# Two token groups through a two-layer encoder trunk: gathered tokens first, dense tokens behind them in plain fp32

## The reference

```python
# layer 0: gMLP over chunks of 128 tokens
u, v = split(gelu(rms_norm(h) @ w_in));  v = rms_norm(v)
h = h + (u * (ws . v + bs)) @ w_out
h = h + peer(rms_norm(h))
k, v = split(rms_norm(h) @ w_kv)                  # shared keys and values
# layer 1: sliding-window attention with sinks and ALiBi
h = h + attention(rms_norm(h) @ w_q, k, v) @ w_o
h = h + peer(rms_norm(h))
y = rms_norm(h)

def peer(x):                                      # 8 heads, 16384 experts of one neuron
    sc = (x @ w_q) . sub_keys                     # 2 halves x 128 keys for each head
    top 16 of each half, their 16 x 16 sums, top 16 of these -> idx, gate = softmax
    return sum over 8 x 16 of gate * gelu(exp_u[idx] . x) * exp_v[idx]
```

## Time and profile before

| | |
|---|---|
| time, median of 3 runs | 3579.42 us (3577.8 to 3583.21) |
| the profiled execution | 3584.95 us, its span 3583.1 us |
| busy: PE, DVE, ACT, POOL | 3009.3, 2532.4, 761.0, 1066.6 us |
| mean granted clock of PE | 0.893 |
| DMA | 1001.05 MB, of it gathers 671.13 MB |
| first and second expert stage, first one-hot to last gather step | 516 to 1735 us, 2336 to 3551 us |

### The profile page before, as it was taken

How to read it: one execution, slowest core, us unless ns; L and a number is a source line. 1 busy time by engine, 2 the same in 40 slices (tenths; PEclk the granted TensorE clock), 3 DMA queues, 4 the chain that set the end, 5 groups by cost and what they waited for, 6 DMA issues and landing times. The chain is left out here.

```text
span 3583.1 us, 48006 instructions
## 1 busy us (share of the span) xinstructions
PE 3009.3 (84%) x17918; PEld 2642.4 (74%) x17918; DVE 2532.4 (71%) x5382; ACT 761.0 (21%) x2270; POOL 1066.6 (30%) x872
## 2 busy tenths in 40 slices
PE   7889769999999997665587988599999999985664
PEld 6789759888878886444574888489888888864453
DVE  3346898777777778676635268987777777777776
ACT  2223212111111111111225232222111111111111
POOL 3233122222222223333344331122222222333331
PEclk9989879999999998777785899799999999987777
DMA  3122359999999999999420122599999999999996
GB/s 131 57 74 76 132 207 368 366 390 384 386 373 386 381 375 350 365 350 359 155 64 1 40 94 76 188 352 354 386 387 385 382 384 389 389 345 353 361 352 227
DMA packets 146430, 1001.05 MB, mean 279 GB/s; under 512 B 16976, under 2 KB 18320, under 8 KB 30816
## 3 DMA queue, kind: packets, MB, share of 16 engines
q0 software_dynamic: 92160, 671.13, 48.7%
q1 hardware_dynamic: 50400, 317.74, 23.3%
q10 hardware_dynamic: 3712, 10.26, 0.8%
HBM read 991.33 MB, written 7.86 MB: 279 GB/s over the span
## 5 line engine op out<-in xcount | busy, mean ns | idle before, releaser
L1100 POOL DMA_INDIRECT gat<-uvg,idxg x640 | 752.6, 1176 | 1879.5 <-DVE acc L1389 1829.5
L585 PE MATMUL bank<-a,V 128*128 128x256 f32 x4096 | 1004.8, 408 | 260.2 <-DVE a L1373 260.2
L1381 DVE CUSTOM_DVE_ANT_0 gat<-gat,xrow 128x1024 f32<-128x1024 f32 x640 | 782.0, 1222 | 556.7 <-DMA gat<-uvg,idxg 552.4
L585 PEld LDWEIGHTS bank<-a,V 128*128 128x128 f32 x4096 | 842.9, 207 | 405.3 <-issue 273.9
L572 PE MATMUL bank<-xd,U 128*128 128x256 f32 x4096 | 954.1, 393 | 0.7 <-DMA U<-uvd 0.7
L572 PEld LDWEIGHTS bank<-xd,U 128*128 128x128 f32 x4096 | 801.0, 198 | 112.5 <-DMA U<-uvd 0.8
L1389 DVE SCALAR_TENSOR_TENSOR acc<-gat,wgt,acc 128x1024 f32<-128x1024 f32 x640 | 819.2, 1280 | 28.3 <-ACT wgt L910 27.9
L908 ACT ACTIVATE act<-dot 128x1 f32<-128x1 f32 x640 | 129.2, 202 | 1850.7 <-DVE dot L1381 1850.4
L559 PEld LDWEIGHTS bank<-B,oneA 128*128 128x128 f16 x4096 | 279.6, 151 | 81.8 <-issue 46.7
L559 PE MATMUL bank<-B,oneA 128*128 128x32 f16 x4096 | 286.0, 246 | 59.7 <-DVE B L1362 37.0
L1064 POOL TENSOR_TENSOR wl<-raw,wh 128x1024 fp32r<-128x1024 f32 x76 | 182.9, 2408 | 364.3 <-ACT wh L856 135.0
(11 more groups left out here) (144 smaller groups left out, 2441.1 us busy)
## 6 DMA issues: line engine op xcount, KB each, us to landing
U<-uvd SPq DMA_DIRECT2D x128, 1024.0 KB, 8.6
V<-uvd SPq DMA_DIRECT2D x128, 1024.0 KB, 8.9
raw<-lin SPq DMA_DIRECT2D x76, 512.0 KB, 3.5
gat<-uvg,idxg POOLq DMA_INDIRECT x640, 8.5
hsp<-h ACTq DMA_DIRECT2D x2, 2304.0 KB, 6.9
hx<-hsp SPq DMA_DIRECT2D x2, 2304.0 KB, 15.4
h<-xT SPq DMA_DIRECT2D x8, 288.0 KB, 7.5
yT<-h SPq DMA_DIRECT2D x8, 288.0 KB, 2.3
```

What stands on the lines that cost most here:

```text
L585: mm = pe.matmul(bank[b][:, TD * (d % 2):TD * (d % 2) + TD], V[:, s, o:o + P], a[:, s, TD * k:TD * k + TD], start=(first and k == 0 and d ...
L1100: pool.indirect_dma_start(gat[:, s % SLOTS, :], None, uvg[l], bass.IndirectOffsetOnAxis(idxg[:, s:s + 1], 0)).then_inc(g_in[s % SLOTS], 16)
L1381: dve.tensor_tensor_reduce(gat[:, s % SLOTS, 0:D], gat[:, s % SLOTS, 0:D], xrow[:, min(s // P, 2), :], 1.0, 0.0, ALU.mult, ALU.add, dot[:, ...
```

## The change

Tokens are split into group g (chunks 2 to 4, the gathered ones, 320 tokens) and group d (chunks 0 and 1, the dense ones, 256 tokens). In each layer group g passes all stages up to its selection first; group d follows. Norms, sums, evacuations and searches are made for each group; each weight tile is loaded twice (`LOADS`). Group g keeps the split into three fp32r products, with 320 columns (`tile_g`). Group d multiplies the raw fp32 weights (`tile_d`), with `xd` as its input. PE makes the rank and index products of the first gathered chunks between dense tiles. Steps of the gathered experts stand at places between stages of group d (`AT`): in the input and mixing stage, behind output tiles, behind key searches and, in layer 1, in the attention of group d. There are 59 and 64 steps ahead of the pair loop (46 before). In the attention of group d DVE scales the probabilities (POOL did). Buffers are laid out anew. Keys and values are made for d and then g before any attention. The core of the diff:

```diff
-SEL_STEPS, HOT_STEPS = 3, 2
-EARLY = SEL_STEPS * (NTC - 1) + HOT_STEPS * LEAD
+AT = (
+    [("two", 4), ("mix", 1), *[(f"add{m}", 1) for m in range(6)], *[(f"top{m}", 1) for m in range(8, HP)],
+     ("sel3", 3), ("sel4", 3), *[(f"hot{m}", 2) for m in range(LEAD)]],
+    [*[(f"att{n}", 1) for n in range(1, 16, 2)], *[(f"add{m}", 1) for m in range(6)],
+     *[(f"top{m}", 1) for m in range(8, HP)],
+     ("sel2", 2), ("sel3", 3), ("sel4", 3), *[(f"hot{m}", 2) for m in range(LEAD)]])
+EARLY = tuple(sum(n for _, n in a) for a in AT)
+LOADS = ["ing", "outg", "pq0g", "ind", "outd", "pq0d", "kvd", "kvg", "qg", "og", "pq1g", "qd", "od", "pq1d"]
...
         def step0(i):
-            return EARLY + i * (NSTEP - EARLY) // NPAIR
+            return EARLY[l] + i * (NSTEP - EARLY[l]) // NPAIR
...
+            def tile_g(name, m, part=None):
+                s = m % 4
+                out = bank[s][:, 0:TG_]
+                pe.wait_ge(lo_done[s], LO[name] + m // 4 + 1)
+                pe.wait_ge(free[s], BASE[name][s] + m // 4)
+                for k in range(DT):
...
+                    pe.matmul(out, whi, xh[:, k, :], start=(k == 0), stop=False)
+                    pe.matmul(out, whi, xl[:, k, :], start=False, stop=False)
+                    mm = pe.matmul(out, wlo, xh[:, k, :], start=False, stop=(k == DT - 1))
+                mm.then_inc(full[s], 1)
+            def tile_d(name, m, x, ready=None):
+                s = m % 4
+                pe.wait_ge(raw_in[s], 16 * (KB[name] + m // 4 + 1))
+                pe.wait_ge(free[s], BASE[name][s] + m // 4)
+                for k in range(DT):
...
+                    mm = pe.matmul(bank[s][:, 0:TD], raw[:, s, P * k:P * k + P], x[:, k, :], start=(k == 0),
+                                   stop=(k == DT - 1))
+                mm.then_inc(full[s], 1)
...
+            def gmlp(grp):                                    # PE
+                for m in range(2 * DT):
+                    tile(f"in{grp}", m, "mix0", xd, (nv_done, DT * APPLY["mix0d"]))
+                    if grp == "g" and m == 3:
+                        norm_sums("n0d")
+                    if grp == "d":
+                        if m == 4:
+                            second_rank(0, 0)
+                        if m == 7:
+                            gathered_index(0, 0)
+                        if m == 10:
+                            second_rank(0, 1)
+                        if m == 13:
+                            gathered_index(0, 1)
...
             def experts(l):
-                expert_scores(l, 0, 0)
-                expert_scores(l, 1, 1)
-                for i, c in enumerate(ORDER):
-                    second_rank(l, i)
...
-                    expert_scores(l, i + 2, i % 2)
+                n = 0
+                for i in range(2 if l else 3, NTC):
+                    expert_scores(l, n, n % 2)
+                    second_rank(l, i)
+                    expert_scores(l, n + 1, (n + 1) % 2)
+                    if i < len(GC):
+                        gathered_index(l, i)
+                    else:
+                        turn(l, i)
+                    n += 2
+                for i in range(n, RING0):
+                    expert_scores(l, i, i % 2)
...
+            attention("g")                                    # PE, layer 1
+            added("og", "n4g", None, None, None)
+            selection(1, "g")
+            for m in range(DT):
+                tile("qd", m, None, xd, (nv_done, DT * APPLY["mix1d"]))
+                if m == 4:
+                    second_rank(1, 0)
+                if m == 7:
+                    gathered_index(1, 0)
+            attention("d")
+            added("od", "n4d", None, xd, None)
+            selection(1, "d", 1)
...
+                    if s == BEFORE_TOP[l] + 2:                # POOL, among the gathers
+                        indices(l, "d")
...
+                if grp == "d":                                # DVE, att_norm
+                    dve.wait_ge(rin_done, u + 1)
+                    for e in range(2):
+                        dve.tensor_scalar(S[0:w, n % SS, e, 0:wk], S[0:w, n % SS, e, 0:wk], rin[0:w, n % SS, e, :],
+                                          None, ALU.mult).then_inc(pn_done, 1)
...
+            normed("n0g", G_MIX0, "g", "mix0")                # DVE, layer 0
+            normed("n0d", G_MIX0, "d")
+            gmlp("g")
+            add_to_h(0, "outg")
+            normed("n2g", G_FFN0, "g", "ffn0")
+            step = best_keys(0, "g", step)
+            step = choose(0, 0, step)
+            step = choose(0, 1, step)
+            steps_at(0, "two")
+            gmlp("d")
+            add_to_h(0, "outd")
+            normed("n2d", G_FFN0, "d")
+            step = choose(0, 2, step)
+            step = best_keys(0, "d", step)
+            for i in (3, 4):
+                step = choose(0, i, step)
+                steps_at(0, f"sel{i}")
+            experts(0)
...
+            attention("g")                                    # DVE, layer 1
+            add_to_h(1, "og")
+            normed("n4g", G_FFN1, "g", "ffn1")
+            normed(None, G_MIX1, "d")
+            step = best_keys(1, "g", step)
+            step = choose(1, 0, step)
+            attention("d")
+            add_to_h(1, "od")
+            normed("n4d", G_FFN1, "d")
+            step = choose(1, 1, step)
+            step = best_keys(1, "d", step)
+            for i in (2, 3, 4):
+                step = choose(1, i, step)
+                steps_at(1, f"sel{i}")
+            experts(1)
```

More of the change, by code:

```diff
@@ new lines, in steps, with span, tops, score_bank @@
+        def steps(l, i):
+            return range(step0(l, i), step0(l, i + 1))
+        UNITS = {grp: [(j, c) for j in range(DT) for c in CHUNKS[grp]] for grp in "gd"}
+        UNIT0 = {"g": 0, "d": len(UNITS["g"])}
+        def span(grp, c):
+            o = TCO[c] - COLS[grp].start
+            return slice(o, o + TCS[c])
+        def tops(l, grp):
+            return 2 * HP * l + (HP if grp == "d" else 0)
+        def score_bank(grp, m):
+            return (4 + m % 4, m // 4) if grp == "g" else (4 + m % 2, m // 2)
@@ new lines, in selection @@
+            def selection(l, grp, mid=None):
+                name = f"pq{l}{grp}"
+                for m in range(HP):
+                    tile(name, m, f"ffn{l}", xd, (nv_done, DT * APPLY[f"ffn{l}d"]))
+                    if m == 0 and grp == "g":
+                        x_rows(l)
+                    if m >= 1:
+                        scores(l, grp, m - 1)
+                    if grp == "d" and m == 2:
+                        second_rank(l, mid)
+                    if grp == "d" and m == 4:
+                        gathered_index(l, mid)
+                scores(l, grp, HP - 1)
@@ L810, in at_tile @@
[L810 to L823 removed]
+                    act.wait_ge(sq_used, (DT - 1) * k + dt - 1)
@@ L1467, in _ @@
-            add_to_h("out", "pq0")
-            stats(2)
-            apply(G_FFN0, h, xf, 2)
-            step = selection(0, step)
+            for m in range(4):
+                high(dve, dve.tensor_copy, "ing", m)
+            normed("n0g", G_MIX0, "g", "mix0")
+            normed("n0d", G_MIX0, "d")
+            gmlp("g")
+            add_to_h(0, "outg")
[3 more added lines that the diff above has]
+            step = choose(0, 1, step)
@@ L1536, in _, with attention @@
-            stats(4)
-            apply(G_FFN1, h, xf, 5)
-            step = selection(1, step)
+                dve.tensor_tensor(xl[:, j, span("g", c)], bank[4 + n % 2][:, 0:TCS[c]],
+                                  xh[:, j, span("g", c)].bitcast(F32), ALU.subtract).then_inc(free[4 + n % 2], 1)
+            def attention(grp):
+                for n in range(len(UNITS[grp]) + 4):
+                    if n < len(UNITS[grp]):
+                        att_max(grp, n)
+                    if 0 <= n - 1 < len(UNITS[grp]):
+                        att_norm(grp, n - 1)
+                    if 0 <= n - 4 and grp == "g":
+                        att_low(n - 4)
+                    if grp == "d":
+                        steps_at(1, f"att{n}")
```

1293 lines of the change are left out of this document (661 added, 632 removed).

## The result

The changed kernel takes 3453.73 us (median of four runs, 3443.51 to 3455.63) against 3579.95 for the kernel before on the same chip: ratio 0.9641, 95% interval 0.9621 to 0.9661. The profiled execution took 3455.63 us.

The account below looks back on a forecast made before the run. Predicted bound: DMA in the expert stage, a chain of waits ahead of it. Gathers -99, U loads +11, layer 0 -4.5, layer 1 +16 sum to -76 us; cut to -55, giving 3530 us from 3584.95, range 3465 to 3595.

Parts of the forecast that it names:

- the price of a gather: Pair loops: each gather moved ahead saves 3.2 us, between 2.74 and 4.05; 31 of them gain 99 us (85 to 122).
- layer 1's head: Layer 1 up to its one-hot stage: 617 us against 600.7 before, so 16 us later.
- the allowance: Whole kernel: for waits a hand layout forgets, the sum of -76 us was cut to -55, between -12 and -100.
- a queue of equal loads: Expert stage: gathers and U and V loads of 1.049 MB each queue on DMA; starting gathers earlier shortens it.
- The prediction's own test: Whole kernel: a gain above 76 us would mean a gather costs its full 4 us in the pair loop.
- U loads given back: Choosing stage: fewer score products run ahead, so three and one more loads fall into the full stage, 11 us lost.
- Layer 0's head: Layer 0 from the start to its one-hot stage: 511.5 us, 4.5 us earlier than 516.
- Linear tiles: Linear stages: gathered tile 3.53 us, dense 3.49, together 7.0 against 6.36; TensorE loses 50 us in all.
- the weights loaded twice: Before the experts: 40 MB more DMA traffic, costed at nothing; without cover 104 us.
- B: Dense half: VectorE's list becomes the bound; slower from a share of 0.77 downward, 3600 us at 0.75; chance 0.17.
- C: Pair loop: does not shrink where TensorE is 0.97 busy, only the last 24 pairs do; 3575 us; chance 0.14.
- D: Dense attention and elsewhere: ScalarE's table changes stall longer than the load itself, 30 us more, 3560 us; chance 0.11.

Follow-up runs that it names:

- few_early: Changed kernel with 41 of the 55 gather steps ahead of the one-hots (19 in layer 0, 22 in layer 1) put back into the pairs: 3565.57 us.
- slots_3: Changed kernel with three gather slots instead of four: 3987.28 us.
- axpy_first: Changed kernel with two VectorE instructions exchanged: the axpy of step s-1 stands ahead of the dot product of step s: 3394.2 us.
- before_axpy: Kernel before the change, with only the exchange of axpy_first (axpy of step s-1 ahead of the dot product of step s): 3443.7 us.
- scores_first: axpy_first with three U products, not one, ahead of the first rank product, and dense-attention gathers at four places of two, not eight of one: 3389.48 us.
- few_early_axpy: Changed kernel with both edits, those of few_early (41 early steps fewer) and axpy_first (the exchange): 3419.29 us.

## Why the prediction was too cautious, step by step

**The steps that failed** are three terms of nearly one size that erred to the same side: the price of a gather (22.5 us too low in all), layer 1's head (23 us) and the allowance (21 us). No one of them explains the miss. The mechanism was right: 13 and 18 gathers left the pair loops, and these gave most of the gain.

**The price of a gather** was put so: "Price of one: by bytes 1.049 MB/382 GB/s = 2.74 us; by the pair's period 3.7 to 4.05 us. I take 3.2, since U and V shrink with nothing." The loops lost 121.5 us over 31 gathers, 3.92 each, near the upper end; layer 1's main pairs came every 16.02 us, not 16.4. (few_early, the one run that moves nothing but gathers, gives 3.5 each, 108 us for 31; what gave the other 13 us is open, and single executions differ by nearly as much.) The reason for 3.2 supposes "a queue of equal loads" at a fixed rate, drawn from a DMA share of 0.98. The share was no ceiling: slots_3 shows that the slots set the pace, axpy_first and before_axpy the same bytes at a higher rate. The row that spoke for it stood in the earlier trace rows: VectorE was idle 556.7 us for gathers. The other half of the circle stood on the page of the kernel before, where GpSimd's gathers waited 1829.5 us for VectorE's own axpy:

```profile
L1100 POOL DMA_INDIRECT gat<-uvg,idxg x640 | 752.6, 1176 | 1879.5 <-DVE acc L1389 1829.5
```

The prediction's own test, "A larger gain than 76 would mean that a gather costs its full 4 us in the loop", pointed the right way, but of the 53 us beyond 76 only 22.5 come from the loops.

The Trainium skill, "Perfetto Trace Analysis", section "Identifying the Most-Contended Engine", says that occupancy misleads for DMA and that throughput should be read instead; section "Engine Utilization", under "Roofline", puts the 16 engines of one core at about 435 GB/s. This case agrees that the share misleads: 0.98 at 382 GB/s, 1.00 at 410; neither main pairs nor tails reached 435 in any run.

**U loads given back**: +11 predicted, +14.5 measured, but as work of TensorE: layer 0's one-hot stage has 1072 records of TensorE instead of 1005 (kernel before, 516.4 to 662.2 us); 64 of the 67 more are two products of 7 us, and scores_first takes them off again. Layer 1 gave none back.

**Layer 0's head** followed the layout within 4 us up to the dense input (gathered input 103.4, gathered selection 254.3, dense input 320 for predicted 102, 253.5, 323.5). Behind it the marks come 8 to 11 us early (dense output 367.9 for 376, third chunk 395.4 for 406.5, key searches 454.5 for 463.5), and the first one-hot stands at 504.1 for 511.5.

**Layer 1's head** took 594.7 us and not the 617 laid out; against the kernel before that is 7 us less where 16 more were predicted, 23 us apart. Ten of these lie ahead of the attention (it begins 88.5 us after the last axpy, not 98.5), while the attention of group g took 94 us for 90, and the stretches between and behind differ by 3 or 4 us either way. Sixteen are the dense attention: 80 us, 4.9 a unit, were assumed and it took 64, the low end of "65 to 100". VectorE's work was priced from the mean of all 40 units, but half of the dense units read one block of keys: 53.33 us for 16 units are 3.3 each, not 4.1.

**The allowance** taken on top failed as well: from a sum of -76 the prediction went to -55 for hand-overs that would be missed. Hardly any showed: loop price (22.5), layer 1's head (23), layer 0's (8), the rest (3), less U (3.5), make the 53 us between the sum, -76.5 unrounded, and -129.6, and the allowance adds 21.

**Linear tiles** came as predicted: three dense tiles take 336.05 to 346.58, 3.51 us each (first row), and seven blocks of a gathered tile 203.90 to 206.98, 0.147 us a product.

```profile
336.05 10.69 PE L499 MATMUL bank<-uv_d,raw 128*128 128x256 f32 x48
346.58 0.59 PE L516 MATMUL bank<-g,ones 128*128 128x256 f32 x2
```

```profile
203.90 0.31 PE L488 MATMUL bank<-xh,wl 128*128 128x320 f32 x1
...
206.98 0.31 PE L488 MATMUL bank<-xh,wl 128*128 128x320 f32 x1
```

DMA moved 1043.13 MB for 1041 predicted, and the weights loaded twice stayed hidden: the dense stretches of the first table have shares of 0.52 to 0.66.

**The rivals.** B fell: VectorE's share in the two dense halves is 0.83 and 0.84 (207 of 250 us, 218 of 260), above its 0.77. C fell: main pairs shrank in both layers, from 17.29 and 17.20 us to 16.42 and 16.02. In layer 1 they arrive next to TensorE's 15.94, and with the axpy first C's limit is what cuts the early steps from 112 to 25 us. D fell. ScalarE in the dense attention:

```profile
2044.12 1.28 ACT L1052 ACT_TABLE_LOAD   x1
2045.41 0.20 ACT L1052 ACTIVATE act<-dot 128x1 f32<-128x1 f32 x1
2045.65 0.29 ACT L1054 ACTIVATE wgt<-act,gateg 128x1 f32<-128x1 f32 x1
2045.96 1.28 ACT L1164 ACT_TABLE_LOAD   x1
2047.26 0.40 ACT L1164 ACTIVATE S_d<-S_d,nm 128x128 f32<-128x128 f32 x1
```

Each load is followed after 0.01 to 0.02 us, and the eight steps with their 16 changes cost 10 us in all (few_early), no more than half the 21 us of the loads themselves. The drain of which the Trainium skill, "ScalarE: Activation LUTs", section "What ACT_TABLE_LOAD costs", speaks does not show here.

## What to carry to other kernels

A DMA queue that is busy all the time is a bound only if its rate is the best that this kernel reaches; where the consumer waits for the load and the load waits for the consumer's slot, what a transfer costs is nearly the round over the slots (3.5 to 3.9 of 4.0 us here), and the first thing to shorten is how long a slot is held after its data have landed. Work moved out of such a loop is worth most of the round's share until the next limit is reached, here TensorE's 15.94 us a pair, so the two remedies do not add up. A sum of terms should not be cut by a general allowance for missed hand-overs; each needs a place and a row.

## What the runs showed of the hardware

The DMA engines' busy share said little of the rate: 0.98 at 382 GB/s and 1.00 at 410 with the same mix of loads. With three slots the share fell to 0.86 and the rate to 320 GB/s. A gather was then at its dot product 7.1 us after its issue, where it took 9.3 with four, but its slot was held 7.4 us instead of 6.4, so the round became only a little shorter (14.8 against 16.0 us). The highest rates of main pairs, 412 to 415 GB/s at a share of 1.00, came in few_early_axpy, which has the exchange and the most gathers in a pair.
